# The last row tile of a hybrid encoder layer: its variance offset, its root and the store of its upper half

## The chip, the cores and the metric

One core of one Trainium2 chip runs the whole kernel. The metric is device time in microseconds (us), the median of several executions. One execution of the kernel before was also taken by the hardware profiler, and all rows below are from it.

## The reference

One layer of a streaming encoder: a layer norm of x, three attention branches with gates, a merge, an output projection, and a second layer norm over `alpha * h + y`. Only the end matters here:

```python
y = merged @ w_out[l]
h = layer_norm(alpha * h + y, ln_g[l], ln_b[l])

def layer_norm(x, g, b):
    mu = jnp.mean(xf, axis=-1, keepdims=True)
    var = jnp.mean(jnp.square(xf - mu), axis=-1, keepdims=True)
    y = (xf - mu) * lax.rsqrt(var + LN_EPS)
    return y * g + b
```

The input is 512 frames by 2048 channels in float32. Mean and variance are taken over the 2048 channels of a frame.

## The kernel before, in words

The 512 frames stand as four row tiles (TT = 4) of 128 partitions by 2048 float32 elements in the buffer `resid`, 1 MB each. A half tile is 1024 columns (BW), 512 KB. Each engine has its own program, and they meet at semaphores only. The order of the work is written out by hand in those programs.

The output projection is cut into products of quarters (G1 to G7). The last product, G4, completes quarter 2 of the columns of tiles 2 and 3. The normalisation of a tile then goes through these steps:

- VectorE adds the last sums (`add_rows`, L2406), takes statistics of 512 columns at a time (`stats_tile`, L2391) and aggregates them to mean and variance (`moments`, L2395).
- VectorE centres: (resid - mean) * ln_g in one instruction per half tile (`centre`, L2401).
- GpSimd makes the reciprocal root in two instructions (`rstd`): variance + LN_EPS (L2851), then that to the power -0.5 (L2854).
- For tiles 0 to 2, ScalarE multiplies by the root in place (`scale`, L1594), and GpSimd stores with a DMA that adds into `out` (`store_tile`, L2859). Much earlier, `out` was filled with ln_b in all rows (L2758), so that the adding store completes the affine step. Tile 2 goes in two halves, tiles 0 and 1 whole.
- Tile 3 is different. After both halves are centred, VectorE waits for the root and does resid * root + ln_b in one instruction per half (L2548). SyncE stores the lower half (L657) and ScalarE's queue stores the upper half (L1692), both with plain DMAs that overwrite what stands in `out`.

GpSimd's order at the end is: roots of tiles 0 and 1, stores of tiles 0 and 1, root of tile 2, store of the lower half of tile 2, store of its upper half, root of tile 3. SyncE's program ends with waits for the two plain stores and for the four adding ones, and the kernel ends when all engines have.

Adding DMAs are issued by GpSimd and go through queue q0; SyncE's plain ones go through q1 and ScalarE's through q10. All three feed the same 16 DMA engines.

Of the kernel before, what the change touches and what calls it, by code (L numbers as in the profile page):

```python
# [26 lines left out]
ALU = mybir.AluOpType  # L27
# [4 lines left out]
D = 2048  # L32
SEQ = 512
MEM = 256
TT = SEQ // P
MT = MEM // P
KT = D // P
BW = 1024
# [5 lines left out]
LN_EPS = 1e-5  # L44
# [61 lines left out]


LN_STEPS, F_STEPS, PRESET_STEPS = 4 * TT, 9, 4
OUT_STEPS = 12 + 4 * TT + 10
OUT_GROUPS = 2  # L110
DOUBLES = BT // 2
OUT_RING = 4
# [53 lines left out]
def program(nc, x, mem, ln_in_g, ln_in_b, rel_table, w_in, b_gate, b_forget, sinks,  # L166
# [3 lines left out]
    out_t = out[0].rearrange("(t p) d -> t p d", p=P)  # L170
# [17 lines left out]
    def at(offset, name, shape, dtype):  # L188
        return nc.alloc_sbuf_tensor_at(name, shape, dtype, offset=base + offset)
# [19 lines left out]
    mv = at(CONST + 2432, "mean_var", [P, TT, 2], F32)  # L209
    small = at(CONST + 2464, "small", [P, 8, TT], F32)  # L210
# [119 lines left out]
    resid = at(R1, "resid", [P, TT, D], F32)  # L330
    g2_row = at(RAW, "ln_g_row", [P, D], F32)
    b2_row = at(RAW + 8192, "ln_b_row", [P, D], F32)
# [18 lines left out]
    with ExitStack() as ctx:  # L351
# [3 lines left out]
        def sem(name):  # L355
            return ctx.enter_context(nc.semaphore(name))
# [34 lines left out]
        var_ready = sem("var_ready")  # L391
        rstd_ready = sem("rstd_ready")
# [7 lines left out]
        pool_step = sem("pool_step")  # L400
# [84 lines left out]
        centred = sem("tile_centred")  # L485
# [3 lines left out]
        last_half = sem("last_half_tiles_ready")  # L489
        halves_stored = sem("last_half_tiles_stored")  # L490
        preset = sem("out_preset")
        out_stored = sem("out_stored")
# [5 lines left out]
        def _(sp):  # L498
# [156 lines left out]
            sp.wait_ge(preset, 16 * TT)  # L655
            sp.wait_ge(last_half, 1)
            sp.dma_start(out_t[TT - 1][:, 0:BW], resid[:, TT - 1, 0:BW]).then_inc(halves_stored, 16)  # L657
            sp.wait_ge(halves_stored, 32)
            sp.wait_ge(out_stored, 16 * TT)


        @block.tensor
# [510 lines left out]
        def _(act):  # L1173
# [140 lines left out]
            for i in range(HC):  # L1314
                for s in range(8):
                    if s in (2, 4):
# [3 lines left out]
                                       scale=1.0 / 16).then_inc(b_q_hi, 1)  # L1320
# [245 lines left out]
            def left_hi(p, d):  # L1566
                if p == G1:
                    act.wait_ge(m_turned, 4 * d + 4)
                else:
                    act.wait_ge(m_summed, d + 1 + (DOUBLES if p in (G2, G6, G7) else 0))  # L1570
                hi, _, unsplit = left_tiles(p, d)
                act.activation(hi, unsplit, ACT.Copy).then_inc(m_hi_ready, 1)
# [18 lines left out]
            def scale(t, cols, done):  # L1591
                act.wait_ge(rstd_ready, TT + t + 1)
                act.wait_ge(centred, done)
                act.activation(resid[:, t, cols], resid[:, t, cols], ACT.Copy, scale=small[:, 3, t:t + 1])\  # L1594
                    .then_inc(scaled, 1)
# [52 lines left out]
            for g in range(OUT_GROUPS):  # L1648
                z = out_pairs[g]
                for n, (p, d) in enumerate(OUT_SEQ[g]):  # L1650
# [10 lines left out]
                    z, x, y, w = out_pairs if g == 0 else out_pairs[1:] + out_pairs[0:1]  # L1661
# [26 lines left out]
            scale(1, slice(0, D), 3)  # L1688
            scale(2, slice(0, BW), 4)
            scale(2, slice(BW, D), 5)  # L1690
            act.wait_ge(last_half, 2)
            act.dma_start(out_t[TT - 1][:, BW:D], resid[:, TT - 1, BW:D]).then_inc(halves_stored, 16)  # L1692


        @block.vector
        def _(dve):
# [45 lines left out]
            steps = Steps(dve, dve_once, LN_STEPS)  # L1742
# [73 lines left out]
            steps = Steps(dve, dve_once, F_STEPS, base=LN_STEPS)  # L1816
            steps.mark(dve.memset(f_zero[:, :], 0.0))
            for s in range(2):
# [6 lines left out]
                                     in1=f_n[:, :], op0=ALU.add, op1=ALU.add)\  # L1825
# [3 lines left out]
                                     op0=ALU.mult, op1=ALU.min).then_inc(f_logit, 1)  # L1829
            dve.wait_ge(f_exp, 3)  # L1830
            steps.mark(dve.scalar_tensor_tensor(out=f_z[:, :], in0=f_z[:, :], scalar=0.0, in1=f_n[:, :],
                                                op0=ALU.min, op1=ALU.subtract))
# [76 lines left out]
            for i in range(HC):  # L1909
                steps = Steps(dve, dve_heads, 3 + TT, i)  # L1910
# [12 lines left out]
                for s in range(8):  # L1923
                    if s in (2, 4):
# [3 lines left out]
                                                 scalar=1.0 / 16, in1=c_q[:, m, :].bitcast(F32),  # L1928
                                                 op0=ALU.mult, op1=ALU.subtract).then_inc(q_ready, 1)
# [126 lines left out]
            steps = Steps(dve, dve_once, PRESET_STEPS, base=LN_STEPS + F_STEPS)  # L2056
# [254 lines left out]

            steps = Steps(dve, dve_once, OUT_STEPS, base=LN_STEPS + F_STEPS + PRESET_STEPS)

# [79 lines left out]
            def moments(t):  # L2393
                steps.settle()
                dve.bn_aggr(mv[:, t, :], stats2[:, t, :, :]).then_inc(var_ready, 1)  # L2395

            def centre(t, cols):
                dve.wait_ge(var_ready, TT + t + 1)
                dve.wait_ge(g2_loaded, 16)
                z = resid[:, t, cols]  # L2400
                return dve.scalar_tensor_tensor(out=z, in0=z, scalar=mv[:, t, 0:1], in1=g2_row[:, cols],  # L2401
                                                op0=ALU.subtract, op1=ALU.mult)
# [50 lines left out]
            z, y, w = out_pairs[1], out_pairs[3], out_pairs[0]  # L2453
            halves = slice(0, BW), slice(BW, D)
            for g in range(OUT_GROUPS):
                for n, (p, d) in enumerate(OUT_SEQ[g]):
                    if g and (p, d) == (G4, 3):
                        centre(1, halves[0]).then_inc(centred, 1)
# [51 lines left out]
                    if (p, d) == (G4, 0):  # L2510
                        for t in range(2):
                            dve.wait_ge(u1_added, t + 1)
                            stats_tile(t, 3)
                            moments(t)
                        centre(0, slice(0, D)).then_inc(centred, 1)
                    if (p, d) == (G4, 3):
                        centre(1, halves[1]).then_inc(centred, 1)
# [20 lines left out]
            steps.settle()  # L2538
            stats_tile(3, 2)
            moments(3)  # L2540
            for half in halves:
                steps.mark(centre(3, half))
            steps.settle()
            dve.wait_ge(rstd_ready, TT + 4)
            dve.wait_ge(b2_loaded, 16)
            for half in halves:
                z = resid[:, 3, half]
                dve.scalar_tensor_tensor(out=z, in0=z, scalar=small[:, 3, 3:4], in1=b2_row[:, half],  # L2548
                                         op0=ALU.mult, op1=ALU.add).then_inc(last_half, 1)
            steps.close()  # L2550


# [1 line left out]
        def _(pool):  # L2554
# [292 lines left out]
            add_to_resid(1, 3, o_c12, st_c22)  # L2847

            def rstd(t):
                pool.wait_ge(var_ready, TT + t + 1)  # L2850
                pool.tensor_scalar(small[:, 2, t:t + 1], mv[:, t, 1:2], LN_EPS, None, ALU.add)\  # L2851
                    .then_inc(pool_step, 1)
                pool.wait_ge(pool_step, 5 + TT + t + 1)
                pool.tensor_tensor(small[:, 3, t:t + 1], small[:, 2, t:t + 1], minus_half[:, :], ALU.pow)\  # L2854
                    .then_inc(rstd_ready, 1)

            def store_tile(t, cols, done):
                pool.wait_ge(scaled, done)
                pool.dma_start(out_t[t][:, cols], resid[:, t, cols], accum_op=ALU.add).then_inc(out_stored, 16)  # L2859

            pool.wait_ge(preset, 16 * TT)
            rstd(0)
            rstd(1)
            store_tile(0, slice(0, D), 1)
            store_tile(1, slice(0, D), 2)
            rstd(2)
            store_tile(2, slice(0, BW), 3)
            store_tile(2, slice(BW, D), 4)
            rstd(3)


# [39 lines left out]
```

## Time and profile before

| | us |
|---|---|
| median of 3 executions | 1841.87 |
| lowest, highest | 1840.96, 1842.37 |
| the profiled execution | 1840.76 |
| its span in the trace | 1838.9 |
| TensorE busy in the span | 1822.7 (99%) |
| last matmuls of the kernel | about 1826 |

The span begins with the first instruction and ends with the last. In the profile's rows the first number is a start from the beginning of the span. A DMA has two times: the issue, which occupies the issuing engine, and the landing, which is when its semaphore says that all is written. The landing is counted from the issue.

### The profile page before, as it was taken

To read this page: it belongs to the slowest core of one execution; us is meant where nothing else is said; L and a number is where in the kernel's file an instruction comes from. 1 tells how busy PE (TensorE), PEld (TensorE's weight loads), DVE (VectorE), ACT (ScalarE), POOL (GpSimd) and SP (SyncE) were. 2 spreads that over 40 slices of the span, in tenths; PEclk is the share of its full clock that TensorE was granted. 3 is DMA by queue.
4 is the path that set the end of the run, shared out by engine and by line. 5 is a ranking of instruction groups with operands and counts; after the bars stand their busy time and mean duration, and the time that the engine had idled before them with its cause. 6 is when DMAs were issued, how large, how long until landed. Compare 5 with 4: busy or idle time off the path is not lost.

```text
span 1838.9 us, 24157 instructions
## 1 busy us (share of the span) xinstructions
PE 1822.7 (99%) x8577; PEld 1513.7 (82%) x8577; DVE 1317.2 (72%) x2086; ACT 863.3 (47%) x1458; POOL 201.9 (11%) x276
## 2 busy tenths in 40 slices
PE   9999999999999999999999999999999999999997
PEld 7888888888888888888888888888888888888885
DVE  5777764887777775566678878878788645566778
ACT  5653332545555554344445555555456333244643
POOL 1111110100212120000000000000001000002222
PEclk9999999999999999999999999999999999999998
DMA  9576676962643433444263451624527544439987
GB/s 330 182 206 177 186 198 214 237 218 66 178 122 94 117 101 110 118 116 140 69 193 106 170 189 53 217 69 161 201 75 285 184 149 149 149 115 238 245 211 176
DMA packets 226470, 299.38 MB, mean 163 GB/s; under 512 B 13585, under 2 KB 140625, under 8 KB 224337
## 3 DMA queue, kind: packets, MB, share of 16 engines
q1 hardware_dynamic: 171824, 188.24, 32.2%
q0 software_dynamic: 54416, 109.51, 22.2%
q8 instruction: 50, 0.82, 0.2%
q10 hardware_dynamic: 144, 0.52, 0.1%
q14 instruction: 36, 0.29, 0.0%
HBM read 247.73 MB, written 50.97 MB: 162 GB/s over the span
## 4 chain that ended last, share of the span: by engine, by line
PE 97%; DVE 1%; DMA 1%; ACT 0%; issue 0%; DVEq 0%; POOL 0%; POOLq 0%; SPq 0%; ACTq 0%
PE acc L668 10%; PE acc L670 10%; PE acc L669 10%; PE scores L863 6%; PE scores L861 6%; PE scores L859 6%; PE acc L863 3%; PE acc L861 3%; PE acc L859 3%; PE transposed L693 3%; PE scores L1104 2%; PE scores L1102 2%; PE scores L1103 2%; PE attended L863 2%; PE attended L861 2%; PE attended L859 2%
## 5 line engine op out<-in xcount | busy, mean ns | idle before, releaser
L1292 ACT ACTIVATE piece_split<-w 128x512 fp32r<-128x512 f32 x448 | 282.9, 633 | 288.4 <-PE scores L863 105.1
L1854 DVE TENSOR_TENSOR piece_split<-w,piece_split 128x512 fp32r<-128x512 f32 x448 | 309.1, 691 | 110.2 <-ACT piece_split L1292 98.5
L1708 DVE TENSOR_TENSOR w_lo<-raw_weights,w_hi 128x1024 fp32r<-128x1024 f32 x181 | 220.3, 1220 | 179.0 <-ACT w_hi L1187 177.7
L668 PE MATMUL acc<-h_hi,w_lo 128*128 128x512 f32 x800 | 319.3, 399 | 0.0
L670 PE MATMUL acc<-h_hi,w_hi 128*128 128x512 f32 x800 | 312.4, 391 | 0.0
L669 PE MATMUL acc<-h_lo,w_hi 128*128 128x512 f32 x800 | 311.7, 390 | 0.0
L1187 ACT ACTIVATE w_hi<-raw_weights 128x1024 fp32r<-128x1024 f32 x181 | 191.2, 1060 | 190.3 <-PE acc L1104 52.2
L670 PEld LDWEIGHTS acc<-h_hi,w_hi 128*128 128x128 f32 x800 | 150.2, 188 | 32.4
L668 PEld LDWEIGHTS acc<-h_hi,w_lo 128*128 128x128 f32 x800 | 150.4, 188 | 29.8 <-issue 1.8
L669 PEld LDWEIGHTS acc<-h_lo,w_hi 128*128 128x128 f32 x800 | 150.6, 188 | 28.5
L859 PE MATMUL scores<-piece_split,h_lo 128*128 128x512 f32 x384 | 149.6, 390 | 0.0
L863 PE MATMUL scores<-piece_split,h_hi 128*128 128x512 f32 x384 | 149.4, 389 | 0.0
L861 PE MATMUL scores<-piece_split,h_hi 128*128 128x512 f32 x384 | 149.4, 389 | 0.0
L859 PE MATMUL acc<-piece_split,h_sums 128*128 128x512 f32 x256 | 99.6, 389 | 0.0
L861 PE MATMUL acc<-piece_split,h_sums 128*128 128x512 f32 x256 | 99.6, 389 | 0.0
L863 PE MATMUL acc<-piece_split,h_sums 128*128 128x512 f32 x256 | 99.6, 389 | 0.0
L861 PEld LDWEIGHTS scores<-piece_split,h_hi 128*128 128x128 f32 x384 | 72.1, 188 | 15.0
L863 PEld LDWEIGHTS scores<-piece_split,h_hi 128*128 128x128 f32 x384 | 72.1, 188 | 14.9
L859 PEld LDWEIGHTS scores<-piece_split,h_lo 128*128 128x128 f32 x384 | 72.1, 188 | 14.9
L861 PEld LDWEIGHTS acc<-piece_split,h_sums 128*128 128x128 f32 x256 | 48.0, 188 | 10.0
L859 PEld LDWEIGHTS acc<-piece_split,h_sums 128*128 128x128 f32 x256 | 48.0, 188 | 10.0
L863 PEld LDWEIGHTS acc<-piece_split,h_sums 128*128 128x128 f32 x256 | 48.0, 188 | 9.9
(447 smaller groups left out, 3675.3 us busy)
## 6 DMA issues: line engine op xcount, KB each, us to landing
w<-in_w_in SPq DMA_DIRECT2D x128, 512.0 KB, 7.4
raw_weights<-in_w_in SPq DMA_DIRECT2D x102, 512.0 KB, 3.9
raw_weights<-in_w_branch SPq DMA_DIRECT2D x48, 512.0 KB, 5.2
raw_weights<-in_w_mem_kv SPq DMA_DIRECT2D x32, 512.0 KB, 5.4
gate<-gate_scratch POOLq DMA_DIRECT2D x12, 1024.0 KB, 6.6
h_sums<-sums_scratch POOLq DMA_DIRECT2D x6, 1024.0 KB, 10.4
gate_scratch<-first_product POOLq DMA_DIRECT2D x12, 512.0 KB, 6.3
out_w_x<-in_w_out POOLq DMA_DIRECT2D x12, 512.0 KB, 8.4
```

Source lines behind the costliest of these rows:

```text
L668: pe.matmul(bank_out, wl, hi[:, k, :], start=first, stop=False)
L669: pe.matmul(bank_out, wh, lo[:, k, :], start=False, stop=False)
L670: return pe.matmul(bank_out, wh, hi[:, k, :], start=False, stop=last)
L693: last = pe.transpose(tp[f % 2][:, col:col + P], src, ident[:, :])
L859: pe.matmul(banks[t][:, :], lo[:, k, tok], wh, start=first and k == 0, stop=False, skip_group_check=True)
L861: pe.matmul(banks[t][:, :], hi[:, k, tok], wl, start=False, stop=False, skip_group_check=True)
L863: last = pe.matmul(banks[t][:, :], hi[:, k, tok], wh, start=False, stop=k == BT - 1, skip_group_check=True)
L1102: pe.matmul(bank_out, lo[:, k, tok], wh, start=k == 0, stop=False)
L1187: act.activation(w_hi[:, slot, :], raw[:, slot, :], ACT.Copy).then_inc(hi_ready, 1)
L1292: act.activation(p_split[:, n % RING, 0, :], sources[p][:, k, :], ACT.Copy).then_inc(pc_hi, 1)
L1708: dve.tensor_tensor(w_lo[:, slot, :], raw[:, slot, :], w_hi[:, slot, :].bitcast(F32), ALU.subtract).then_inc(lo_ready, 1)
L1854: dve.tensor_tensor(p_split[:, n % RING, 1, :], sources[p][:, k, :], p_split[:, n % RING, 0, :].bitcast(F32), ALU.subtract).then_inc(pc_lo, 1)
```

## The change

The variance offset of tile 3 moves from GpSimd to VectorE. GpSimd raises it to the power -0.5 before it issues the store of the upper half of tile 2, and VectorE waits for that root before it centres tile 3. The upper half of tile 3 is centred first, then scaled by ScalarE, and stored by GpSimd with an adding DMA as tiles 0 to 2 are. The lower half is centred second and keeps its path: one VectorE instruction and SyncE's plain store.

```diff
@@ SyncE
-            sp.wait_ge(halves_stored, 32)
-            sp.wait_ge(out_stored, 16 * TT)
+            sp.wait_ge(halves_stored, 16)
+            sp.wait_ge(out_stored, 16 * (TT + 1))
@@ ScalarE
             scale(2, slice(BW, D), 5)
-            act.wait_ge(last_half, 2)
-            act.dma_start(out_t[TT - 1][:, BW:D], resid[:, TT - 1, BW:D]).then_inc(halves_stored, 16)
+            scale(3, slice(BW, D), 6)
@@ VectorE
+            def offset_variance(t):
+                dve.wait_ge(var_ready, TT + t + 1)
+                dve.tensor_scalar(small[:, 2, t:t + 1], mv[:, t, 1:2], LN_EPS, None, ALU.add).then_inc(var_ready, 1)
...
             moments(3)
-            for half in halves:
-                steps.mark(centre(3, half))
+            offset_variance(3)
+            dve.wait_ge(rstd_ready, TT + 4)
+            centre(3, halves[1]).then_inc(centred, 1)
+            steps.mark(centre(3, halves[0]))
             steps.settle()
-            dve.wait_ge(rstd_ready, TT + 4)
             dve.wait_ge(b2_loaded, 16)
-            for half in halves:
-                z = resid[:, 3, half]
-                dve.scalar_tensor_tensor(out=z, in0=z, scalar=small[:, 3, 3:4], in1=b2_row[:, half],
-                                         op0=ALU.mult, op1=ALU.add).then_inc(last_half, 1)
+            z = resid[:, 3, halves[0]]
+            dve.scalar_tensor_tensor(out=z, in0=z, scalar=small[:, 3, 3:4], in1=b2_row[:, halves[0]],
+                                     op0=ALU.mult, op1=ALU.add).then_inc(last_half, 1)
@@ GpSimd
             def rstd(t):
-                pool.wait_ge(var_ready, TT + t + 1)
-                pool.tensor_scalar(small[:, 2, t:t + 1], mv[:, t, 1:2], LN_EPS, None, ALU.add)\
-                    .then_inc(pool_step, 1)
-                pool.wait_ge(pool_step, 5 + TT + t + 1)
+                if t < TT - 1:
...
+                else:
+                    pool.wait_ge(var_ready, TT + t + 2)
                 pool.tensor_tensor(small[:, 3, t:t + 1], small[:, 2, t:t + 1], minus_half[:, :], ALU.pow)\
                     .then_inc(rstd_ready, 1)
...
             store_tile(2, slice(0, BW), 3)
+            rstd(3)
             store_tile(2, slice(BW, D), 4)
-            rstd(3)
+            store_tile(3, slice(BW, D), 5)
```

## Rows read from the trace of the kernel before

**Rows 1.** The page: busy time, share and instructions of each engine.
```profile
PE 1822.7 (99%) x8577; PEld 1513.7 (82%) x8577; DVE 1317.2 (72%) x2086; ACT 863.3 (47%) x1458; POOL 201.9 (11%) x276
```

**Rows 2.** Busy time by stretch: PE, PEld, DVE, ACT, POOL, clock, DMA share, GB/s.
```profile
1816.00:1817.00 1.00, 1.00 (x6) 0.81 (x5) 1.00 (x2) 0.42 (x1) 0.69 (x1) 1.00 0.00 0
1817.00:1818.00 1.00, 1.00 (x6) 0.83 (x5) 1.00 (x2) 0.00 (x0) 0.00 (x0) 1.00 1.37 131
...
1826.00:1827.00 1.00, 0.01 (x1) 0.00 (x0) 1.00 (x2) 0.93 (x1) 0.00 (x0) 1.00 0.90 188
...
1837.00:1838.00 1.00, 0.00 (x0) 0.00 (x0) 0.00 (x0) 0.00 (x0) 0.00 (x0) 0.50 0.25 98
```

**Rows 3.** The chain that ended last, its end: start, us, what.
```profile
1828.70 0.86 POOL out L2859
...
1829.95 1.08 POOLq L351
...
1831.55 1.28 DVE resid L2548
```

**Rows 4.** SyncE's waits after 1830: us in total, times, longest.
```profile
SPq L659 <- DMA out<-resid: 2.5, 1, 2.5
SPq L351 <- DMA out<-resid: 2.4, 1, 2.4
```

**Rows 5.** VectorE in order of time: start, us, line, operation, xcount.
```profile
1828.24 0.26 DVE L2395 BATCH_NORM_AGGREGATE mean_var<-out_bn_stats 128x2 f32<-128x24 f32 x1
1828.54 2.48 DVE L2401 SCALAR_TENSOR_TENSOR resid<-resid,mean_var,ln_g_row 128x1024 f32<-128x1024 f32 x2
1831.55 2.48 DVE L2548 SCALAR_TENSOR_TENSOR resid<-resid,small,ln_b_row 128x1024 f32<-128x1024 f32 x2 [0.53 <-DVE resid L2401]
```

**Rows 6.** GpSimd in order of time, from the root of tile 2.
```profile
1823.75 0.57 POOL L2854 TENSOR_TENSOR small<-small,minus_half 128x1 f32<-128x1 f32 x1
1827.22 0.92 POOL L2859 DMA_DIRECT2D out<-resid  x1 [2.90 <-ACT resid L1594]
1828.70 0.86 POOL L2859 DMA_DIRECT2D out<-resid  x1 [0.56 <-ACT resid L1594]
1829.27 0.63 POOL L2851 TENSOR_SCALAR small<-mean_var 128x1 f32<-128x1 f32 x1
1829.99 1.47 POOL L2854 TENSOR_TENSOR small<-small,minus_half 128x1 f32<-128x1 f32 x1
```

**Rows 7.** ScalarE and SyncE in order of time.
```profile
1825.78 1.15 ACT L1594 ACTIVATE resid<-resid,small 128x1024 f32<-128x1024 f32 x1 [4.53 <-DVE resid L2401]
...
1834.06 0.38 ACTq L1692 DMA_DIRECT2D out<-resid  x1
...
1832.91 0.34 SPq L657 DMA_DIRECT2D out<-resid  x1
```

**Rows 8.** DMA from 1815 on: packets, MB, share of 16 engines; then issues.
```profile
q0 software_dynamic: 576, 3.15, 74.9%
q1 hardware_dynamic: 144, 0.52, 5.4%
q10 hardware_dynamic: 144, 0.52, 5.4%
...
out<-resid SPq DMA_DIRECT2D x1, 512.0 KB, 4.0
out<-resid ACTq DMA_DIRECT2D x1, 512.0 KB, 4.1
```

**Rows 9.** DMA, 1828.6 to 1831 (the issue), then 1834.5 to 1835 (queue).
```profile
out<-resid POOLq DMA_DIRECT2D x1, 512.0 KB, 7.0
...
q0 software_dynamic: 17, 0.03, 31.7%
```

**Rows 10.** Small VectorE operations, whole kernel: busy us, mean ns.
```profile
L2395 DVE BATCH_NORM_AGGREGATE mean_var<-out_bn_stats 128x2 f32<-128x24 f32 x4 | 1.1, 264 | 0.1
...
L1721 DVE MEMSET neg_max<- 128x8 f32 x1 | 0.1, 65 | 0.0
```

More of the change, by code:

```diff
@@ L108 @@
 LN_STEPS, F_STEPS, PRESET_STEPS = 4 * TT, 9, 4
-OUT_STEPS = 12 + 4 * TT + 10
+OUT_STEPS = 12 + 4 * TT + 9
 OUT_GROUPS = 2
@@ L2849, in rstd @@
             def rstd(t):
-                pool.wait_ge(var_ready, TT + t + 1)
-                pool.tensor_scalar(small[:, 2, t:t + 1], mv[:, t, 1:2], LN_EPS, None, ALU.add)\
-                    .then_inc(pool_step, 1)
-                pool.wait_ge(pool_step, 5 + TT + t + 1)
+                if t < TT - 1:
+                    pool.wait_ge(var_ready, TT + t + 1)
+                    pool.tensor_scalar(small[:, 2, t:t + 1], mv[:, t, 1:2], LN_EPS, None, ALU.add)\
+                        .then_inc(pool_step, 1)
+                    pool.wait_ge(pool_step, 5 + TT + t + 1)
+                else:
+                    pool.wait_ge(var_ready, TT + t + 2)
                 pool.tensor_tensor(small[:, 3, t:t + 1], small[:, 2, t:t + 1], minus_half[:, :], ALU.pow)\
```

## The prediction

> **What bounds the kernel now.** I read the page's engine shares first: TensorE is busy 1822.7 of 1838.9 us [rows 1]. Then the stretches near the end: from 1826 on TensorE does nothing [rows 2], so the change lives in the last 12.9 us and can win or lose there alone. Everything ahead of 1826 keeps its order.
>
> Next the chain of waits. It ends in GpSimd's store issue at 1828.70, GpSimd held for 1.08 us, and VectorE's last pass from 1831.55 [rows 3]. The timelines fill this in. The aggregate of tile 3 ends at 1828.50, the two centrings run to 1831.02 (1.28 us each, the second starting 1.20 after the first), the last two passes run 1831.55 to 1834.03 [rows 5]. GpSimd takes 0.63 us for the offset and 1.47 for the power, while the same power took 0.57 for tile 2 [rows 6]. So the last root is slow, and it ends at 1831.46, when both centrings are over. The plain stores go out at 1832.91 and 1834.06 [rows 7] and land 4.0 and 4.1 us later [rows 8], at 1836.9 and about 1838.15. SyncE's waits agree: 2.5 us from the end of its issue at 1833.25 to 1835.75, then 2.4 more to 1838.15 [rows 4]. The first of them is the adding store of tile 2's upper half, issued 1828.70 and landed 7.0 later, at 1835.7 [rows 6, 9]. The span ends 0.75 us after the last landing.
>
> The chain names engines. The DMA rows tell of a second limit beside it. The adding queue q0 has nothing at 1816 to 1817 and is full from 1817 on [rows 2]. It is drained at about 1834.9: in 1834.5 to 1835 only 0.03 MB of it is left [rows 9]. In the 23.9 us from 1815 it held the 16 engines for 74.9%, that is 17.9 us for its 3 MB, with no pause between 1817 and 1834.9. One adding half tile (six of them) costs 17.9 / 6 = 2.98 us of all DMA engines. A plain half tile costs 5.4% of 23.9 = 1.29 us [rows 8]. The moved bytes are the same, the price 2.3 times as high.
>
> **The change part by part, the engines.** The clock starts at the aggregate's end, 1828.50.
>
> - The offset on VectorE: the trace has no such instruction there. It lies between a memset of 128x8 (0.065) and the aggregate (0.264) [rows 10]. I take 0.20, start 1828.54, end 1828.74. It replaces GpSimd's 0.63.
> - GpSimd has finished the issue for tile 2's lower half at 1828.14 [rows 6], so it stands ready. With 0.10 for the semaphore the power starts at 1828.84. VectorE now waits, so nothing holds GpSimd and I take tile 2's 0.57: end 1829.41, where it was 1831.46.
> - VectorE waits 0.75 us for it. Behind this wait stand both centrings, the last pass and through it SyncE's store. Semaphore 0.09 (1831.46 to 1831.55 before): upper centring 1829.50 to 1830.78, lower to 1831.98, last pass of the lower half 1832.02 to 1833.30, SyncE's issue 1833.38. That is 0.47 later than 1832.91. One pass of 1.20 is gone from VectorE.
> - ScalarE scales the upper half: start 0.09 after the centring, 1.15 us [rows 7], so 1830.87 to 1832.02. Nothing else is queued there.
> - GpSimd's issue follows a scaling 0.29 later: 1832.31, where the upper half's store went out at 1834.06. On its way it passes the store of tile 2's upper half, which now stands behind the root and goes out at about 1829.45, 0.75 later than 1828.70.
>
> So the last issue moves from 1834.06 to 1833.38. If stores landed as before, 4.1 us after the issue, the end would come 0.68 us earlier.
>
> **The DMA engines.** The delay of tile 2's upper half to 1829.45 costs nothing. A first packet follows an issue by about 1.4 us (issue 1815.77, nothing before 1817 [rows 2]), so it is ready at 1830.9, and the queue ahead of it (2.5 MB, 5 x 2.98 = 14.9 us from 1817.2) is busy until 1832.1. The cover is 1.2 us.
>
> The new adding store is ready at 1832.31 + 1.4 = 1833.7, also before q0 runs dry at 1834.9. The queue thus never pauses, and issuing earlier buys nothing. Left after 1834.9 are one adding half at 2.98 and one plain half at 1.29, where before there were two plain halves at 1.29. The work grows by 2.98 - 1.29 = 1.69 us. The DMA engines were busy without a pause to 1837 before, only the tail is thin (0.25 at 1837 to 1838 [rows 2]). If all of the extra work shows, the last landing goes from 1838.15 to 1839.84. If the plain half slips entirely into gaps of the adding one, the end is 1834.9 + 2.98 = 1837.9, plus 0.8 from a nearly dry queue to the landing (as 1834.9 to 1835.7 for the store before), 1838.7: +0.55. The bounds are thus +0.55 and +1.69 as long as q0 itself stays full. I take +1.6, near the upper end, because q0's share was full while it ran alone and leaves little to slip into.
>
> Removing SyncE's and ScalarE's waits and one plain issue costs or gives under 0.1 us, hidden behind the landing.
>
> **Sum.** Span 1838.9 + 1.6 = 1840.5, profiled execution 1840.76 + 1.6 = 1842.4. The median of the shown runs stands 1.11 above the profiled execution, so the forecast is 1841.87 + 1.6 = 1843.5. A step of 0.2%, 3.7 us, is about what a measurement of this kernel can tell from no change. The forecast is under it: no change that shows, with a lean to slower.
>
> **A rule of the Trainium skill against rows.** The power took 1.47 us beside two centrings and 0.57 beside an add that reads PSUM [rows 6]. In the Trainium skill, "SBUF — State Buffer", section "Who interferes with whom", a VectorE instruction with two SBUF inputs shuts out a GpSimd instruction that reads SBUF for its whole length. By that rule, the trace agrees; it is the part of the change that works. The same page, section "SBUF: two separate sides", warns that GpSimd's DMAs need the shared port to write descriptors and stall behind some VectorE operations. That is the third rival below.
>
> **Rivals.**
>
> 1. The adding store overlaps well and the shorter chain shows. The last issue is earlier by 0.68; with full overlap on the DMA engines the end lies between -0.7 and +0.6. [...] Against it: one plain half moved at over twice the rate of an adding one, and they use the same engines. Time: about 1841.9 (1841.2 to 1842.5).
> 2. The change doesn't do what it says for the root: GpSimd is still issuing the lower half of tile 2 when the offset is ready. The cover is 1828.14 to 1828.84, 0.7 us. If the issue came 1 us later, VectorE would start its centrings 0.3 later; while q0 is the bound even this hides, since the new store has 1.2 us of room (1833.7 to 1834.9). Time: 1843.5 to 1844.
> 3. Slower: the descriptors of GpSimd's stores are shut out by VectorE. Tile 2's upper store would be issued at 1829.45 just as the centring starts, and VectorE runs two-input passes nearly back to back until 1833.30. Held until then, it starts at 1833.4 + 1.4 = 1834.8; q0 has run dry at 1832.1, and behind it stand two adding halves and one plain, 2 x 2.98 + 1.29 = 7.25, so the end of data is 1842.0 and the landing about 1842.6 with a tail of 0.6. That is +4.4: 1846.3. It decides from the point at which the held issue outlasts the cover of 1.2 us. Against it: the same store was issued at 1828.70 in 0.86 us beside a centring that ran from 1828.54 [rows 5, 6], no longer than the 0.92 of the one before. The page gives its warning for modes with both port pairs, and infers that a two-input operation takes the reading side alone.
>
> **Chances.** The forecast, +0.8 to +2.5: 0.60. Rival 1: 0.25. Rival 2: 0.05. Rival 3: 0.05. Something before 1826 moved by other placement of instructions, either way: 0.05. The likeliest case alone gives 1842.7 to 1844.4. The range adds rival 1 down to 1841.2 and the spread of the medians (1840.96 to 1842.37 over three executions, about 0.7 each way), and stops at 1845.0 short of rival 3. Faster by over 0.2%, below 1838.2, needs more than any term here offers: 0.03. Slower by over 0.2%, above 1845.6, is rival 3 and part of the unnamed: 0.06. Within: 0.91.
>
> **What would show it.** The offset on VectorE takes 0.06 to 0.27 us. The last power takes about 0.57 and ends near 1829.4. The upper centring starts near 1829.5, ScalarE's scaling near 1830.9, GpSimd's last issue near 1832.3, SyncE's near 1833.4. The adding queue shows no pause from 1817 to beyond 1837. The last store to land is GpSimd's, 7 us or more after its issue, at about 1839.8, while the plain one lands near 1837.5 to 1838.5. I am wrong if the adding store lands before 1838.2 (rival 1), if the power is again over 1 us, or if a store issue on GpSimd takes over 1.5 us or q0 pauses near 1832 (rival 3).

## The result, and the profile after

The changed kernel takes 1844.36 us (median of 19 runs, 1842.54 to 1845.75), the kernel before 1840.95 in the same comparison. The ratio is 1.0016, with a 95% interval of 1.0010 to 1.0023: slower by 1.8 to 4.2 us. One of the kernel before's 19 runs took 2623.51 us and is left out of the ratio. This is a loss, and its middle, 0.16%, is still inside the 0.2% that was called no change. The forecast was 1843.5. The profiled execution took 1843.25 us with a span of 1841.4, so 2.5 us more span.

The page first. The adding queue carries one half tile more, and ScalarE's queue q10 is gone.

```profile
span 1841.4 us, 24158 instructions
PE 1823.7 (99%) x8577; PEld 1514.3 (82%) x8577; DVE 1316.0 (71%) x2086; ACT 863.2 (47%) x1459; POOL 201.0 (11%) x276
q0 software_dynamic: 54560, 110.03, 22.3%
```

The timelines of the changed kernel's end, VectorE, then GpSimd, ScalarE and SyncE; they answer to [rows 5 to 7].

```profile
1828.39 0.26 DVE L2394 BATCH_NORM_AGGREGATE mean_var<-out_bn_stats 128x2 f32<-128x24 f32 x1
1828.69 0.15 DVE L2398 TENSOR_SCALAR small<-mean_var 128x1 f32<-128x1 f32 x1
1829.53 2.48 DVE L2404 SCALAR_TENSOR_TENSOR resid<-resid,mean_var,ln_g_row 128x1024 f32<-128x1024 f32 x2 [0.69 <-POOL small L2860]
1832.05 1.28 DVE L2551 SCALAR_TENSOR_TENSOR resid<-resid,small,ln_b_row 128x1024 f32<-128x1024 f32 x1
...
1828.94 0.56 POOL L2860 TENSOR_TENSOR small<-small,minus_half 128x1 f32<-128x1 f32 x1 [0.66 <-DVE small L2398]
1829.46 0.85 POOL L2865 DMA_DIRECT2D out<-resid  x1
1832.36 0.84 POOL L2865 DMA_DIRECT2D out<-resid  x1 [2.05 <-ACT resid L1594]
...
1830.91 1.15 ACT L1594 ACTIVATE resid<-resid,small 128x1024 f32<-128x1024 f32 x1 [2.36 <-DVE resid L2404]
...
1833.41 0.34 SPq L657 DMA_DIRECT2D out<-resid  x1
```

The power takes 0.56 us instead of 1.47 and ends at 1829.50 instead of 1831.46. Every issue stands within 0.05 us of its forecast. The last matmul ended 0.17 us later in this trace than in that of the kernel before, so counted from there the issues came 0.1 us earlier than forecast. The engines did what was worked out; the rest is in the stores. The DMA answers, from 1815 to the end (queues, and by issue the time to landing), and SyncE's waits after 1830, which stand last, answer to [rows 4, 8]:

```profile
q0 software_dynamic: 720, 3.67, 77.3%
q1 hardware_dynamic: 144, 0.52, 5.0%
...
out<-resid SPq DMA_DIRECT2D x1, 512.0 KB, 5.9
```

The new adding store alone, from the answer for 1831 to 1834:

```profile
out<-resid POOLq DMA_DIRECT2D x1, 512.0 KB, 6.1
```

```profile
SPq L659 <- DMA out<-resid: 4.7, 1, 4.7
SPq L351 <- PEq L351: 1.8, 1, 1.8
SPq L351 <- DMA out<-resid: 0.8, 1, 0.8
```

SyncE waits to 1838.45 for the adding store, to 1839.3 for its own plain one (1833.41 + 5.9), and then 1.8 us more for the other engines. Before, this last wait was 0.5 us. The span ends 2.1 us after the last landing, not 0.75.

What SyncE waits for stands under the program's end, line 351, where each engine's closing instruction is a DRAIN. The answer for that line gives durations in ns and starts. First the kernel before, then the changed one.

```profile
L351 POOLq DRAIN  x1: 8142/8142/8142, 1829.9 to 1829.9; - x1
L351 SPq DRAIN  x1: 7/7/7, 1838.4 to 1838.4; - x1
```

```profile
L351 PEldq DRAIN  x1: 4267/4267/4267, 1822.0 to 1822.0; - x1
L351 POOLq DRAIN  x1: 8532/8532/8532, 1832.3 to 1832.3; - x1
L351 SPq DRAIN  x1: 7/7/7, 1839.5 to 1839.5; - x1
```

A DRAIN's record can begin while earlier instructions of its engine still run: GpSimd's begins at 1829.95 in the kernel before, and its power ran to 1831.46. So its end is what counts. GpSimd's DRAIN ends at 1838.1 in the kernel before, 0.3 us ahead of SyncE's own, so nobody waits for it. In the changed kernel it ends at 1840.9, 1.3 us behind SyncE's, and sets the end.

### The profile page after: what moved, and what is told of

Same layout as the page of the kernel before. It is cut to its first block, busy times and chain, and to the rows that moved or that the text cites. A ratio compares the mean times of both kernels' runs of the same rounds, so it can differ in the third digit from the quotient of the medians.

```text
span 1841.4 us, 24158 instructions
## 1 busy us (share of the span) xinstructions
PE 1823.7 (99%) x8577; PEld 1514.3 (82%) x8577; DVE 1316.0 (71%) x2086; ACT 863.2 (47%) x1459; POOL 201.0 (11%) x276
## 4 chain that ended last, share of the span: by engine, by line
PE 97%; DVE 1%; DMA 1%; issue 0%; ACT 0%; SPq 0%; POOL 0%; ACTq 0%; DVEq 0%
PE acc L668 10%; PE acc L670 10%; PE acc L669 10%; PE scores L859 6%; PE scores L861 6%; PE scores L863 6%; PE acc L861 3%; PE acc L859 3%; PE acc L863 3%; PE transposed L693 3%; PE scores L1102 2%; PE scores L1103 2%; PE scores L1104 2%; PE attended L861 2%; PE attended L859 2%; PE attended L863 2%
## 5 line engine op out<-in xcount | busy, mean ns | idle before, releaser
L859 PEld LDWEIGHTS scores<-piece_split,h_lo 128*128 128x128 f32 x384 | 72.1, 188 | 14.9
## 6 DMA issues: line engine op xcount, KB each, us to landing
h_sums<-sums_scratch POOLq DMA_DIRECT2D x6, 1024.0 KB, 10.4
```

Source lines behind the costliest of these rows:

```text
L859: pe.matmul(banks[t][:, :], lo[:, k, tok], wh, start=first and k == 0, stop=False, skip_group_check=True)
```

## The experiments

TensorE's last matmul ends between 1825.5 and 1827.7 in the traces below, so a span alone compares badly. The "tail" is the span less that end: 12.9 us before (1838.9 - 1826.0), 15.2 in the changed kernel (1841.4 - 1826.2). Landings below are counted from there too, and each is its issue plus its time to landing. Medians are in us, ratios against the kernel before, with 95% intervals. The kernel before was run again in each comparison, with medians of 1840.95 to 1841.30.

| kernel | median | ratio | q0's last landing | last plain landing | GpSimd's DRAIN ends after q0's landing | tail |
|---|---|---|---|---|---|---|
| before | 1840.95 | 1 | 9.7 | 12.2 | 2.34 | 12.9 |
| changed | 1844.36 | 1.0016 (1.0010-1.0023) | 12.3 | 13.2 | 2.38 | 15.2 |
| changed, again | 1844.83 | 1.0019 (1.0010-1.0029) | 13.9 | 14.2 | 2.38 | 16.8 |
| upper half plain | 1841.36 | 1.0000 (0.9990-1.0009) | 9.5 | 12.0 | 2.34 | 12.4 |
| adding store alone | 1846.05 | 1.0026 (1.0017-1.0036) | 14.5 | 10.3 | 2.38 | 17.4 |
| early root alone | 1841.60 | 1.0002 (0.9992-1.0011) | 10.1 | 12.5 | 2.34 | 13.0 |
| GpSimd issues a plain store | 1843.57 | 1.0012 (1.0002-1.0021) | 12.0 | 10.7 | 2.38 | 14.9 |
| no lower store | 1843.97 | 1.0015 (1.0006-1.0024) | 13.4 | none | 2.38 | 16.3 |
| halved stores, on before | 1841.35 | 1.0002 (0.9993-1.0011) | 9.6 | 12.1 | 2.42 | 12.5 |
| halved stores, on changed | 1843.42 | 1.0011 (1.0002-1.0020) | 13.9 | 14.1 | 2.46 | 16.6 |
| offset on VectorE alone | 1841.33 | 1.0001 (0.9992-1.0010) | 9.5 | 12.0 | 2.34 | 12.4 |
| tile 2's upper half plain | 1840.65 | 1.0001 (0.9992-1.0010) | 6.7 | 12.0 | 2.30 | 12.4 |
| the same, last half in quarters | 1841.69 | 1.0003 (0.9994-1.0012) | 6.8 | 12.5 | 2.30 | 12.9 |

**Upper half plain.** On the changed kernel:

```diff
             scale(3, slice(BW, D), 6)
+            act.wait_ge(scaled, 5)
+            act.dma_start(out_t[TT - 1][:, BW:D], resid[:, TT - 1, BW:D]).then_inc(halves_stored, 16)
...
-            store_tile(3, slice(BW, D), 5)
```

> The changed kernel, but tile 3's upper half is stored by a plain DMA from ScalarE's queue as soon as it is scaled (ln_b is left out of that half). Root, centring and scaling are those of the changed kernel. Theory D (the adding store is the cost twice: on the DMA engines, and because GpSimd's closing DRAIN ends about 2.35 us after q0's last landing): q0's last landing is again tile 2's upper half, near 1835.4, the drain ends near 1837.8, the last landing of all is a plain one near 1838.1, span 1838.6 to 1839.1, 2.3 to 2.8 below the changed kernel. Theory E (the early root and the later lower half are what costs): span stays above 1840.5.

The tail is 12.4, the median 3.0 below the changed kernel's and equal to that of before. Only the kind and the queue of one store differ (it was issued 5.9 us after the last matmul, 0.3 earlier than the adding one), so the loss sits there. Which of the two it is, kind or queue, this run can't tell. The span forecast of 1838.6 to 1839.1 was missed (1840.2), mainly because the last matmul ended 1.6 us later in this trace: counted from the last matmul, 12.6 to 13.1 was forecast and 12.4 measured.

**Early root alone, adding store alone.** On the kernel before, the two parts of the change:

```diff
# early root alone
+            offset_variance(3)
+            dve.wait_ge(rstd_ready, TT + 4)
             for half in halves:
                 steps.mark(centre(3, half))
             steps.settle()
-            dve.wait_ge(rstd_ready, TT + 4)
...
+            rstd(3)
             store_tile(2, slice(BW, D), 4)
-            rstd(3)
# adding store alone
+            scale(3, slice(BW, D), 6)              # ScalarE, for its plain store
...
+            centre(3, halves[1]).then_inc(centred, 1)
+            steps.mark(centre(3, halves[0]))
...
             store_tile(2, slice(BW, D), 4)
             rstd(3)
+            store_tile(3, slice(BW, D), 5)
```

> The early root alone: offset on VectorE, power before tile 2's upper store, both centrings after it, then both halves finished by VectorE and stored plainly as before. The plain stores are issued near 1833.4 and 1834.6, 0.5 later than before. Theory D: q0 is dry near 1835 as before, the DMA engines then have two plain halves, last landing 1838.2 to 1838.7, drain end 1837.8, span 1838.9 to 1839.4. Theory E: as the changed kernel, 1841.

> The adding store alone: offset and power stay on GpSimd behind tile 2's upper store, VectorE centres without waiting, ScalarE scales tile 3's upper half when the root is there, GpSimd stores it with the adding DMA. Theory D: the store is issued near 1833.1, 0.8 later than in the changed kernel and still before q0 is dry at 1835, so the landing (1838.5), the drain (1840.9) and the span (1841.4) stay as in the changed kernel within 0.4. Theory E: back near 1839.

The early root alone does nearly as said: plain stores issued 0.35 us later (0.5 forecast), tail 13.0, no loss that shows. The adding store alone loses as the changed kernel does or more, 1846.05; my "within 0.4" was wrong. In the changed kernel the adding store was issued 1.05 us before SyncE's plain one. Here both go out together, at 1832.63 and 1832.60, and the plain one wins:

```profile
out<-resid SPq DMA_DIRECT2D x1, 512.0 KB, 3.5
out<-resid POOLq DMA_DIRECT2D x1, 512.0 KB, 7.6
```

It lands after 3.5 us, the adding one after 7.6, and that one carries the DRAIN. Between 1834.5 and 1835 the queues' answer has one line:

```profile
q1 hardware_dynamic: 52, 0.21, 103.3%
```

No packet of q0 started there, though its store had been issued 1.9 us before, and by the prediction's 1.4 us its packets were due at 1834.0. Whether they were late or stood behind the plain store's is not shown. Whether the early root is thus worth 1 to 2 us beside an adding store is not settled: the two ratios' intervals overlap.

**GpSimd issues a plain store.** The kernel before, with the upper half's plain store moved from ScalarE's queue to GpSimd's:

```diff
-            act.wait_ge(last_half, 2)
-            act.dma_start(out_t[TT - 1][:, BW:D], resid[:, TT - 1, BW:D]).then_inc(halves_stored, 16)
...
+            pool.wait_ge(last_half, 2)
+            pool.dma_start(out_t[TT - 1][:, BW:D], resid[:, TT - 1, BW:D]).then_inc(out_stored, 16)
```

> The kernel before, but tile 3's upper half, finished by VectorE, is stored by a plain DMA that GpSimd issues on q0 instead of ScalarE. The bytes and their price on the DMA engines stay. Theory Q (only the work on the DMA engines counts, end is last landing plus 0.75): landing 1838.2 to 1838.5, span 1839 to 1839.3. Theory D: the landing is the same but is now q0's last, so the drain ends 2.35 later, near 1840.7, and the span is 1841.1 to 1841.5. Theory F (the drain takes a fixed 7.7 to 8.5 us from GpSimd's last issue, whatever lands): issue ends near 1835, drain end 1842.7 to 1843.5, span 1843 to 1844.

The issue, its landing and GpSimd's DRAIN in this trace:

```profile
1835.45 0.64 POOL L2869 DMA_DIRECT2D out<-resid  x1 [2.87 <-DVE resid L2546]
...
out<-resid POOLq DMA_DIRECT2D x1, 512.0 KB, 3.7
...
L351 POOLq DRAIN  x1: 6120/6120/6120, 1835.4 to 1835.4; - x1
L351 SPq DRAIN  x1: 7/7/7, 1839.4 to 1839.4; - x1
```

It lands at 1839.15, early as a plain store does, and the DRAIN ends at 1841.5, 2.4 later, while SyncE had been done since 1839.4. (The span forecast of 1841.1 to 1841.5 was missed at 1842.1, the last matmul ending 1.1 us later than in the trace before.) The bytes and their price did not change, yet the kernel is slower by 0.12% and the tail 2.0 us longer. That rules out "only work on the DMA engines counts". A fixed time after GpSimd's last issue falls too: from the end of that issue to the end of the DRAIN it is 5.5 us here, 7.7 in the changed kernel and 9.1 with the adding store alone, while the time from q0's last landing is 2.3 to 2.5 in all 13 traces. What is left of its spread follows the number of stores that GpSimd issues at the end: 2.30 us with three, 2.34 with four, 2.38 with five, 2.42 with six, 2.46 with seven, the kind making no difference.

So the queue alone, with a plain store, costs nearly what the whole change does: ratios 1.0012 and 1.0016, with intervals that overlap. That doesn't make the adding kind free, because here the store was issued 8.3 us after the last matmul and in the changed kernel at 6.2. An estimate: a plain store of GpSimd's issued at 6.2, landing after the 4.9 us of "upper half plain", would put the end of the DRAIN at 13.5 and the tail at 14.0. That would make 1.1 us of queue, and 1.2 to 2.8 of kind up to the two tails of the changed kernel. No run has such a store, so how the loss divides is not shown.

**No lower store.** The changed kernel without SyncE's plain store; the lower half of tile 3 is left out of the output.

> The changed kernel without the plain store of tile 3's lower half (that half of the output is left out). Theory Q (the work on the DMA engines sets the end): 1.3 us of work is gone, and the last landing goes from 1839.3 to q0's at 1838.4: span falls by 0.9 to 1.3. Theory D (GpSimd's closing DRAIN, 2.35 us after q0's last landing, sets it): the adding store was served first anyway, so the span falls by 0.0 to 0.5 against the last matmul.

The median is the changed kernel's within 0.4 us. The plain store, the last to land, costs nothing that shows there. The tail of this one trace, 16.3, is longer than the forecast, because the adding store, alone on the DMA engines, took 7.2 us to land:

```profile
1833.50 0.84 POOL L2863 DMA_DIRECT2D out<-resid  x1 [2.05 <-ACT resid L1592]
...
out<-resid POOLq DMA_DIRECT2D x1, 512.0 KB, 7.2
```

**The changed kernel again.**

> The changed kernel once more, for a second trace of it. Theory D: GpSimd's closing DRAIN again ends 2.3 to 2.5 us after q0's last landing and is the last thing to end; the landing itself may move with the slowest of the 16 DMA engines, 12.3 to 13.4 after the last matmul, the tail with it, 15.2 to 16.3.

The store took 7.7 us in this trace where it took 6.1 in the first, with its issue at the same place (6.2 after the last matmul). The DRAIN followed 2.38 us behind both. The tail was 16.8, above the upper end. The two halves of tile 2 had landed 1.2 us later as well (7.9 and 10.4 after the last matmul, 6.7 and 9.2 in the first trace), so the delay was there before the new store. The adding store's landing is thus the uncertain term, 12.3 to 13.9, and the first trace showed a quick case.

**Halved stores.** Tiles 0 and 1 centred, scaled and stored in halves, on the kernel before and on the changed one:

```diff
-            store_tile(0, slice(0, D), 1)
-            store_tile(1, slice(0, D), 2)
+            store_tile(0, slice(0, BW), 1)
+            store_tile(0, slice(BW, D), 2)
+            store_tile(1, slice(0, BW), 3)
+            store_tile(1, slice(BW, D), 4)
```

> The kernel before, with tiles 0 and 1 centred, scaled and stored in halves, so that the adding queue starts 0.8 us earlier. Theory D with a full queue: all four adding tiles' landings move 0.8 earlier, q0's last to 8.9 us after the last matmul (9.7 before), the drain with it to 11.3, the plain stores' last landing to 11.4 to 12.2: the tail after the last matmul, 12.9, falls to 12.1 to 12.9. Rival (the queue is limited by the late issue of tile 2, not by its backlog): no change.

> The changed kernel with the same halves. Theory D: q0's last landing, 12.3 us after the last matmul, moves to 11.5, the drain and the span with it: tail 15.2 falls to 14.4, still above the kernel before's 12.9. Rival (the queue is limited by the issue of the last store at 6.2 after the last matmul): no change.

The first issue did come 0.86 us earlier, and on the kernel before q0's last landing moved by 0.1 (9.7 to 9.6). On the changed kernel it was 13.9, as in that kernel's second trace, and the tail forecast at 14.4 was 16.6. The rivals were right, and the stretches of the first trace show why (PE, PEld, DVE, ACT, POOL, clock, DMA share, GB/s):

```profile
1828.00:1829.00 1.00, 0.00 (x0) 0.00 (x0) 0.93 (x3) 0.28 (x1) 0.72 (x2) 1.00 1.01 94
1829.00:1830.00 1.00, 0.00 (x0) 0.00 (x0) 1.00 (x2) 0.00 (x0) 1.00 (x2) 1.00 0.48 70
```

In the kernel before the same two stretches read 168 and 127 GB/s. Here the queue runs thin before tile 2's lower half, issued at 1827.38, brings new packets. What the earlier start gains is lost again there: from then on tile 2's issue, not the backlog, sets q0's last landings.

**Offset on VectorE alone.** The kernel before with `offset_variance(3)` and no wait for the root.

> The kernel before with the variance offset of tile 3 on VectorE and nothing else: VectorE does not wait, the power stays behind tile 2's upper store. Theory D: VectorE starts its centrings 0.2 later, the power slips between the two centrings (as GpSimd's offset did before) and ends near 4.4 us after the last matmul instead of 5.5, so the last passes and both plain stores go out 0.2 to 0.4 earlier. q0's landing and the drain (12.1) stay, so the tail, 12.9, falls by at most 0.3. Rival: the power still waits for both centrings, and everything is 0.2 later.

```profile
1829.06 2.48 DVE L2405 SCALAR_TENSOR_TENSOR resid<-resid,mean_var,ln_g_row 128x1024 f32<-128x1024 f32 x2
1831.57 2.48 DVE L2553 SCALAR_TENSOR_TENSOR resid<-resid,small,ln_b_row 128x1024 f32<-128x1024 f32 x2
...
1829.70 1.07 POOL L2862 TENSOR_TENSOR small<-small,minus_half 128x1 f32<-128x1 f32 x1
```

The power starts under the first centring and ends at 1830.77, before the second one does (1831.54), so the last passes follow the centrings at once. The plain stores go out 0.4 earlier. The last landing comes only 0.2 earlier (12.2 to 12.0). The tail reads 0.5 shorter, because the span also ends 0.4 us after that landing instead of 0.7. All six variants with a tail of 13.0 or less end 0.4 us after their last landing, so 0.3 us of what their tails gain on the kernel before is not the stores'. The median shows no difference.

**A version with one adding store less.** VectorE finishes tile 2's upper half right after the offset, and SyncE stores it plainly; the second kernel also cuts the last half in quarters.

```diff
-            for half in halves:
-                centre(2, half).then_inc(centred, 1)
+            centre(2, halves[0]).then_inc(centred, 1)
+            steps.mark(centre(2, halves[1]))
...
+            offset_variance(3)
+            dve.wait_ge(rstd_ready, TT + 3)
+            dve.wait_ge(b2_loaded, 16)
+            z = resid[:, 2, halves[1]]
+            dve.scalar_tensor_tensor(out=z, in0=z, scalar=small[:, 3, 2:3], in1=b2_row[:, halves[1]],
+                                     op0=ALU.mult, op1=ALU.add).then_inc(last_half, 1)
```

> One adding store fewer instead of one more: VectorE finishes tile 2's upper half too (1.2 us more on it, right after the offset, while GpSimd makes the root), and SyncE stores it plainly; tile 3 in two plain halves as before. Theory D: q0's last landing is tile 2's lower half, 6.5 to 7.3 after the last matmul, drain end 8.9 to 9.7, no longer near the end. The last plain store is issued near 8.8 (8.05 before) and finds free DMA engines: landing 11.8 to 12.3, tail 12.4 to 13.0 against 12.9 before and 15.2 for the changed kernel. Theory Q alone (work on the engines): 1.7 less work, tail 11.2 to 12. Theory E (only the engines' chain counts): 0.75 later than before, 13.6.

> The kernel above with the last plain half cut in two quarters, finished and stored one after the other. Theory D: the last issue is near 8.9 and only 256 KB are behind it, so its landing is 0.4 to 0.7 earlier than above, the tail 11.9 to 12.5: below the kernel before by 0.4 to 1.0. Rival (the fixed part of a store counts, not its bytes): as above or 0.2 later.

GpSimd's DRAIN now ends at 1834.9 (1828.8 + 6.1), 3.2 us ahead of SyncE's at 1838.1. The last plain store, issued 1.0 us later than before, landed after 3.0 us instead of 4.1, which pays for the longer VectorE chain. The tail is 12.4 and the median 1840.65, lowest of all, with a ratio of 1.0001 (0.9992 to 1.0010): no gain that these runs can tell. Quarters do not help: the tail is 12.9, above the 11.9 to 12.5 that was forecast, and the rival was nearer. The 256 KB stores took 3.2 and 3.3 us to land, no less than the 3.0 of the 512 KB one in their place. The first line below is the median of two, 3.9 and 2.7.

```profile
out<-resid SPq DMA_DIRECT2D x2, 512.0 KB, 3.3
out<-resid ACTq DMA_DIRECT2D x2, 256.0 KB, 3.3
```

The first of the two kernels also has a third slow power, begun under VectorE's pass over tile 2's upper half:

```profile
1828.67 1.28 DVE L2550 SCALAR_TENSOR_TENSOR resid<-resid,small,ln_b_row 128x1024 f32<-128x1024 f32 x1
1828.84 1.54 POOL L2868 TENSOR_TENSOR small<-small,minus_half 128x1 f32<-128x1 f32 x1 [0.85 <-DVE small L2400]
```

## Why the prediction was right, and where it was not

- **The engines' steps** held. Offset 0.15 us (0.20 assumed), power 0.56 (0.57), centring from 1829.53 (1829.50), ScalarE at 1830.91 (1830.87), GpSimd's last issue at 1832.36 (1832.31), SyncE's at 1833.41 (1833.38).
- **A shorter chain buys nothing** held: the last issue came 0.65 us earlier and the kernel is slower. Counted from the last matmul it came 0.82 earlier. Rival 1 is out, and rival 2 did not occur: GpSimd had ended its issue at 1828.28, and the power began at 1828.94. Rival 3 is out: the store of tile 2's upper half was issued in 0.85 us beside the centring and landed at 1835.4.
- **The adding store's price on the DMA engines** was forecast as the only reason. The plain store in its place removes the loss, but it left GpSimd's queue too, and a plain store on that queue costs 0.12% by itself. How much of the loss is the price is not shown, and it had the wrong consequence. I let the extra 1.69 us lengthen the landing of the last of all stores; that moved by 1.15 (1838.2 to 1839.35), or by 1.0 and 2.0 against the last matmul in the two traces. And I had the adding store land last, near 1839.8, with the plain one near 1838. It was the other way round: the adding one at 1838.5, the plain one held behind it to 1839.3.
- **The step that failed is "the span ends 0.75 us after the last landing".** It held for the kernel before and not after. The end has two ways: SyncE's waits, and GpSimd's DRAIN, which ends 2.3 to 2.5 us after q0's last landing. Before, they ended 0.3 us apart (1838.1 and 1838.4), which hid the second. The change moves q0's last landing by +2.57 against the last matmul (9.74 to 12.31), the slack takes 0.3 of it, and the tail grows by 2.3. In the second trace of the changed kernel it is +4.1, less the slack, and 3.9 in the tail. The ratio says 2.9 (1.8 to 4.2), the two medians 3.4. My 1.6 is just under this interval. That the number came near is in part luck: in the first trace the landing grew by 1.0 where I had 1.6, and the end after it by 1.35 where I had nothing. The range held because its upper end lay at 1845.0, for reasons that did not name the DRAIN.
- **A row was misread.** The 1.08 us "POOLq L351" of [rows 3] was taken for GpSimd held at its power. It is the start of that DRAIN, which stands in the chain under the program's closing line.
- **"The queue thus never pauses"** held in the changed kernel, where the new store was issued 3.0 us before tile 2's upper half had landed. In "adding store alone", where the store was issued 0.7 us later, q0 did pause.
- **The slow power was misread in part.** I put 1.47 us down to two centrings [rows 5, 6]. The first had ended at 1829.82, before the power began at 1829.99. It began 0.25 us after the second, and ended 0.44 after the second's end. With the offset on VectorE alone it began 0.65 us into the first centring, took 1.07, and ended 0.43 after the end of that one, although the second was running by then. In "tile 2's upper half plain" it took 1.54 us, and ended 0.43 after the VectorE pass under which it had begun. With no pass beside it, it took 0.56. So its length is what is left of the pass under which it begins, plus 0.43. By the rule of the Trainium skill ("SBUF — State Buffer", "Who interferes with whom"), which shuts it out for the length of a VectorE instruction with two SBUF inputs, the traces agree.

## What to carry to other kernels

At the end of a kernel, count each store to the moment when its issuer's closing DRAIN ends, not to its landing: here GpSimd's came 2.3 to 2.5 us later, where SyncE and the rest were done 0.4 to 0.7 after theirs. So give the last stores to SyncE's or ScalarE's queue, and let GpSimd's be the early ones. An adding store saves an engine pass of 1.2 us and costs 2.3 times the DMA time; here, as the last of a full queue, it lost, and how much of that is its kind and how much its queue is open. And when two ways to the end stand 0.3 us apart, name both before you forecast from one.

## What the runs showed of the hardware

- GpSimd's closing DRAIN ended 2.30 to 2.46 us after the last landing on q0 in 13 traces, for adding and plain stores alike, and 0.04 us later for each further store of GpSimd's at the end (three to seven of them).
- GpSimd's power of 128x1 took 0.56 us alone. Begun under a VectorE pass with two inputs in SBUF, it ended 0.43 or 0.44 us after the end of that pass, which made it 1.07 to 1.54 us, and the next pass behind it did not hold it.
- The same adding store of 512 KB took 6.1, 7.7 and 7.2 us from issue to landing in three traces with the same issue point, in the last of them with nothing beside it.
- A plain store issued 1.05 us behind an adding one landed after 5.9 and 6.9 us in two traces; issued together with it, after 3.5, and the adding one then after 7.6. With the adding queue drained, three plain half tiles took 2.6, 2.7 and 3.0 us, and two quarter tiles 3.2 and 3.3.
